# Sample index scores in four column groups, and two gate tiles moved from the sample steps into the index stage

## The reference, cut to what matters

```python
isc = jnp.einsum('bqhd,bkd->bqhk', qib, k_idx).astype(jnp.float32) * (IDX_DIM ** -0.5)
isc = jnp.einsum('bqhk,bqh->bqk', jax.nn.relu(isc), wib.astype(jnp.float32)) * (IDX_HEADS ** -0.5)
...
vals, idx = lax.top_k(isc, topk)
...
gates = jax.nn.sigmoid(gate_logit.reshape(b, t, N_BRANCH, D_MODEL))
merged = jnp.sum(gates * y, axis=2)
```

## Time and profile before

| | |
|---|---|
| median of 3 runs | 2609.43 us (2607.01 to 2613.8) |
| the profiled execution | 2608.09 us, its span 2606.2 us |
| PE busy | 2493.3 us, 96% of the span, 17084 matmuls |
| DVE, ACT, POOL busy | 1040.1, 566.1, 63.1 us |
| chain that ended last | PE 87%, DMA 6%, DVE 3%, ACT 2% |
| mean granted clock of PE | 0.988 of full |

### The profile page before, as it was taken

How to read it: one execution, slowest core, us unless ns; L and a number is a source line. 1 busy time by engine, 2 the same in 40 slices (tenths; PEclk the granted TensorE clock), 3 DMA queues, 4 the chain that set the end, 5 groups by cost and what they waited for, 6 DMA issues and landing times.

```text
span 2606.2 us, 40922 instructions
## 1 busy us (share of the span) xinstructions
PE 2493.3 (96%) x17084; PEld 2095.9 (80%) x17084; DVE 1040.1 (40%) x2388; ACT 566.1 (22%) x1262; POOL 63.1 (2%) x100
## 2 busy tenths in 40 slices
PE   7999999999999899999999999999999999999998
PEld 6999997656666589999989999965566665999997
DVE  3455202203676435554016660112066854266501
ACT  3000003114544322000021001120235442310101
POOL 0000000000012100000000000000000120000000
PEclk8999999999999999999999999999999999999998
DMA  8566421542369544665642232225414783323321
GB/s 300 186 226 216 165 89 51 143 136 70 110 224 298 166 148 162 227 225 176 219 142 89 98 120 89 94 67 139 130 61 159 254 283 129 130 73 122 109 89 69
DMA packets 299559, 389.92 MB, mean 150 GB/s; under 512 B 33677, under 2 KB 245385, under 8 KB 299378
## 3 DMA queue, kind: packets, MB, share of 16 engines
q1 hardware_dynamic: 281538, 339.52, 38.9%
q0 software_dynamic: 10752, 38.93, 4.6%
q10 hardware_dynamic: 7088, 8.87, 0.9%
HBM read 377.66 MB, written 9.62 MB: 149 GB/s over the span
## 4 chain that ended last, share of the span: by engine, by line
PE 87%; DMA 6%; DVE 3%; ACT 2%; SPq 1%; issue 1%; ACTq 0%; DVEq 0%; POOL 0%; POOLq 0%
PE PS L665 25%; PE PS L711 13%; PE PS L791 12%; PE PS L845 8%; PE PS L1037 4%; PE PS L592 3%; DMA QR<-w_ada 3%; PE PS L648 3%; PE PS L632 2%; PE PS L745 2%; PE PS L734 2%; PE PS L996 2%; PE PS L1059 2%; PE PS L1051 2%; PE PS L966 1%; PE PS L1006 1%
## 5 line engine op out<-in xcount | busy, mean ns | idle before, releaser
L711 PE MATMUL PS<-BIG,RING 128*128 128x192 f32 x2112 | 345.8, 326 | 0.0
L711 PEld LDWEIGHTS PS<-BIG,RING 128*128 128x128 f32 x2112 | 343.0, 190 | 1.5 <-issue 1.4
L791 PE MATMUL PS<-RING,H 128*128 128x384 f32 (+1 forms) x960 | 307.2, 482 | 0.0
L791 PEld LDWEIGHTS PS<-RING,H 128*128 128x128 f32 x960 | 181.8, 190 | 121.0 <-issue 0.6
L845 PE MATMUL PS<-H,RING 128*128 128x384 f32 x672 | 224.3, 488 | 0.0
L665 PE MATMUL PS<-OT,RING 128*128 128x192 f32 x1216 | 222.5, 326 | 0.0
L665 PE MATMUL PS<-H,RING 128*128 128x192 f32 x1216 | 213.8, 329 | 0.0
L665 PE MATMUL PS<-OT,QR 128*128 128x192 f32 x1216 | 210.0, 326 | 0.0
L665 PEld LDWEIGHTS PS<-H,RING 128*128 128x128 f32 x1216 | 199.0, 191 | 5.6 <-issue 5.4
L665 PEld LDWEIGHTS PS<-OT,RING 128*128 128x128 f32 x1216 | 201.8, 190 | 0.0
L665 PEld LDWEIGHTS PS<-OT,QR 128*128 128x128 f32 x1216 | 199.7, 190 | 0.0
(11 more groups left out here) (242 smaller groups left out, 3122.0 us busy)
## 6 DMA issues: line engine op xcount, KB each, us to landing
RING<-ffn_w_in SPq DMA_DIRECT2D x80, 1024.0 KB, 7.2
QR<-w_ada SPq DMA_DIRECT2D x66, 1024.0 KB, 9.4
RING<-w_in SPq DMA_DIRECT2D x64, 768.0 KB, 6.0
RING<-ffn_w_out SPq DMA_DIRECT2D x32, 768.0 KB, 4.6
RING<-ffn_w_out SPq DMA_DIRECT2D x32, 640.0 KB, 5.9
QKT<-cache_sb_k SPq DMA_DIRECT2D x16, 768.0 KB, 6.1
QR<-cache_sb_v POOLq DMA_DIRECT2D x16, 768.0 KB, 4.9
QKT<-cache_fox_k SPq DMA_DIRECT2D x16, 768.0 KB, 6.1
```

Source lines behind the costliest of these rows:

```text
L711: mm = pe.matmul(PS[:, m + 2 * g, 0:HALF], w[:, k, m * P:(m + 1) * P], HID[:, half * k2 + k, GROUP[g]], start=(half == 0 and k == 0), stop ...
L791: mm = pe.matmul(PS[:, n % 3, 0:width], H[:, k, tt * P:(tt + 1) * P], w[:, k, :], start=(k == 0), stop=(k == KD - 1))
```

## The change

`QIP` shrinks from 640 to 128 columns a head: only the 32 query columns of each pair are kept. The four pairs no longer add up in PSUM: each writes 32 PSUM partitions of its own (rows 32 bp to 32 bp + 32), with `start=True, stop=True`. The number of MATMULs stays 64 a layer. The result is the same 128 rows by 528 keys in the same banks.

Gate tiles 6 and 7 (`GATE_SCORE`) are now computed in the index stage, before heads 2 and 3 and behind their waits for the ReLU; ACT takes them after the ReLUs of heads 1 and 2. `prompt_scores(0)` comes after head 3, and behind a wait for tile 7 to be taken. All later tiles have numbers two higher in the prompt stage, in the same places; the sample steps have seven tiles instead of nine, in steps 0, 1, 2, 3, 5, 12 and 19 instead of 0, 1, 2, 3, 4, 6, 11, 17 and 22. `ROUND_S` and the loads stay as they are.

```diff
@@ -60,8 +60,9 @@
 GATE_FIRST = [0, 1, 2]
 GATE_INDEX = [3, 4, 5]
-GATE_PROMPT = [[6, 7, 8], [9, 10], [11], [12], [13], [14]]
-GATE_STEP = dict(zip((0, 1, 2, 3, 4, 6, 11, 17, 22), range(15, 24)))
+GATE_SCORE = [6, 7]
+GATE_PROMPT = [[8, 9, 10], [11, 12], [13], [14], [15], [16]]
+GATE_STEP = dict(zip((0, 1, 2, 3, 5, 12, 19), range(17, 24)))
@@ -188,7 +189,7 @@
-        QIP = qr(o, IH * 640).rearrange("p (h c) -> p h c", h=IH); o += IH * 640
+        QIP = qr(o, IH * P).rearrange("p (h i c) -> p h i c", h=IH, i=4); o += IH * P
@@ -909,14 +910,15 @@
                     if h >= 2:
                         pe.wait_ge(relu_ready, l * 6 + (h + 1))
+                        gate_tile(GATE_SCORE[h - 2], h - 2, 0)
                     for half in range(2):
                         for bp in range(4):
-                            mm = pe.matmul(PS[:, 4 + 2 * (h % 2) + half, 0:264], QIP[:, h, bp * P:(bp + 1) * P],
-                                           KIT[:, bp, half * 264:(half + 1) * 264], start=(bp == 0), stop=(bp == 3))
+                            mm = pe.matmul(PS[32 * bp:32 * bp + 32, 4 + 2 * (h % 2) + half, 0:264], QIP[:, h, bp, :],
+                                           KIT[:, bp, half * 264:(half + 1) * 264], start=True, stop=True)
                     mm.then_inc(is_ready, 1)
-                    if h == 2:
-                        prompt_scores(0)
-
+
+                pe.wait_ge(gate_taken, l * 24 + GATE_SCORE[-1] + 1)
+                prompt_scores(0)
@@ -1295,7 +1297,7 @@
-                        dst = QIP[s, h, :].rearrange("p (i c) -> p i c", c=160)[:, :, NT * par:NT * par + NT]
+                        dst = QIP[s, h, :, NT * par:NT * par + NT]
@@ -1320,6 +1322,8 @@
                           ACT.Relu, scale=1 / 16).then_inc(relu_ready, 1)
+                        if n in (3, 4):
+                            take_gate(GATE_SCORE[n - 3], n - 3)
```

## The result

The changed kernel takes 2631.76 us (median of 4 runs, 2625.38 to 2633.28) beside 2609.19 us for the kernel before on the same chip: ratio 1.0079, 95% interval 1.0058 to 1.0101. So it is slower by about 21 us, where 9 us was forecast and 2628 us was the end of the range. The profiled execution took 2633.28 us against 2608.09.

A forecast was written before the change was run, and what follows sets the result against it. The prediction took PE as the bound (87% of the chain). Terms 1 to 5 gave +2.1 us and term 6 +6.8, so +8.9 on 2608.09; with 1.3 for the runs' median, 2618 us, range 2606 to 2628.

The forecast's parts named there:

- The scores: Index stage: index scores in column groups take 0.9 us a head, 4.2 us a layer instead of 14.5.
- Term 1: Index stage: two tiles brought in, shorter scores and a 4.1 us wait for the ReLU; +4.25 us a layer.
- Term 2: Steps 4 to 7: uncovered top-k rounds delay `output` by 3.05 us in steps 5 and 7; +1.5 us a layer.
- Term 3: Steps 11 to 13: a tile covers step 12's round and mask, step 11's round shows; -0.5 us a layer.
- Term 4: Step 22: without its tile it takes 4.54 us instead of 8.21, like step 23; -3.7 us a layer.
- Term 5: Transfers in the sample steps: some stall saved at step 12, some added in steps 13 to 18; -0.5 us a layer.
- Term 6: PE's clock falls behind new pauses in the index stage and steps 5 and 7; +3.4 us a layer, +6.8 in all.
- Rival A: Forecast mechanics with the clock falling in the index stage and most step pauses; 2613 to 2625 us, chance 0.50.

The follow-up runs named there:

- e14: Changed kernel with discarded MATMULs filling the pauses of the index stage, of steps 5 and 7 and of the end; ratio 1.0022 to the kernel before.
- e4: Changed kernel with 12 discarded MATMULs put into the index stage's pause; ratio 1.0061 to the kernel before.
- e5: Changed kernel with 8 discarded MATMULs put into the pauses of steps 5 and 7; ratio 1.0057 to the kernel before.
- e2: Changed kernel with the top-k rounds of steps 4 and 6 moved under tiles in steps 0, 1 and 5; ratio 1.0033 to the kernel before.
- e16: Changed kernel run once more, unedited; ratio 1.0080 to the kernel before.
- e1: Changed kernel with tile 6 placed ahead of the wait for head 0's ReLU; ratio 1.0023 to the kernel before.
- e10: Changed kernel with tile 6 ahead of the ReLU wait and sample-step tiles in steps 0, 1, 2, 3, 4, 6, 22; ratio 0.9976 to the kernel before.
- e11: Changed kernel with the tile of step 19 moved to step 22; ratio 1.0073 to the kernel before.
- e12: Changed kernel with discarded MATMULs ahead of the values in step 22, in step 23 and after it; ratio 1.0069 to the kernel before.
- e6: Kernel before with the four column groups alone, no tile moved; ratio 0.9998 to the kernel before.
- e15: As e10, but with the seventh sample-step tile in step 17 instead of 22; ratio 0.9986 to the kernel before.

## Why the prediction was wrong, point by point

**The scores, right.** 0.9 us a head in column groups, 4.2 us in all: 1.99 us for two heads and 1.10 for each of the others, 4.2.

**Term 1, the wait: right in mechanism, 0.25 short.** A wait of 4.1 us forecast, 4.18 measured, released by the ReLU. Without the clock the stretch grows by 4.5 us (e14, e4) instead of 4.25.

**Term 2, the uncovered rounds: right.** Steps 4 to 7 are 29.9 us with the clock held up (e5, e14) where 1.5 on top of 28.7 make 30.2. The pause was 2.98 for 3.05. e2 shows it from the other side.

**Term 3: not resolved.** -0.3 / +0.5 for -0.5 in the first profile; over the eight profiles steps 8 to 13 are 34.6 to 35.9 us, 35.3 in the mean, beside 35.5 and 35.3 before.

**Term 4: the first step that failed.** Step 22 was priced by its look-alike, step 23, as if it waited for nothing else. It took 5.65 us in layer 0 instead of 4.54, held by the mask's transfer through DVE, and 6.26 in layer 1; its pause of 2.56 us was followed in layer 0 by 17 us at 0.50 instead of the 7 to 10 that the kernel before has there (layer 1: 3 and 7 us). Of 3.7 us a layer 0.5 and 1.1 were left in this profile, and less in others: in e16 the end is 20.5 and 21.1 us, longer than before, and over the six kernels that have the same end (changed, e16, e1, e2, e4, e5) it is 19.8 in the mean beside 19.7, with 0.6 us won in the branch products. I had looked at the clock only behind the three pauses that I had found, and not at those that a tile taken out leaves at the end.

**Term 5: right in the mean.** -0.8 / -1.2 in steps 14 to 21 of the first profile, 44.9 us in the mean of the eight beside 45.1 and 45.9: -0.6 for -0.5. But the view behind it was too mild. A tile there is worth about 2 us, not 4.6; e10 and e11 show it. For the change itself this costs little, because it has as many tiles in steps 8 to 21 as before, two. The prediction calls 351 GB/s the ceiling; the 389 GB/s from 718.3 to 722.0 show that more is possible, for some us at least.

**Term 6, the clock: the step that failed most.** Mechanism, places and sign were right, and the number of falls nearly so: 4.7 a kernel by the term (two, and 0.67 of four), 5.2 by the traces (14 of 14, and 19 of 24 of the short ones), six in the first profile. The size of a fall was not: I took 1.4 us in the index stage and 1.5 in the steps, from stretches of 3.3 us at 0.50. Measured in the first profile: 2.9 us in the index stage (8.36 for 5.43) and 2.7 and 2.6 in steps 5 and 7, with the clock at 0.50 in all of the 5.5 to 5.9 us read; in the mean of all profiles 2.6 and 2.2. That makes 16 us in the first profile and 12 in the mean, where the term has 6.8. The rows of before had longer falls too, at the ends of the sample steps; I read the six short ones and put the others into the upper end (+12) without weight. The Trainium skill (TensorE: Matmul & The Clock Gate, HAM oscillation) tells of a kernel in which the clock fell again behind every wait; by that, all six fall. Of the pauses here 33 of 38 did: a mean of 5.2 a kernel, no farther from my 4.7 than from six, and neither number makes 12 us without the larger price.

Put together: terms 1 to 5 gave +2.1, and e14, which takes most of the clock out, measures +5.7; the missing gain of term 4, 0.25 us a layer of term 1 and the two falls named below fill that. The clock has the rest, 15 us between e14 and the changed kernel: about 12 are term 6 at its true size, and about 3 are at the end of the sample steps (e12), where the prediction had no new fall. Rival A was the right case, with a price for the clock of little over half and nothing for the end.

What stays open: e14 still has falls at 723 and 2007, behind a pause of 2.0 us before the sample steps that the kernel before has as well and that brings none there. The fills aren't needed for it: e6 and e11, which have none, show the same fall in both layers, and the changed kernel and e16 in neither. Over all 14 profiles this pause brought 12 falls of 28. What decides between them isn't known, nor what decides between a fall of 1.5 us and one of 2.6.

## What to carry to other kernels

Before work is taken off the engine that bounds a kernel, look at what the other engines do under it: here a tile was the cover of two top-k rounds, and a score was long enough to hide a ReLU chain. A pause that is left on TensorE costs its own length and, behind it, up to 3 us more at half clock; put work that is ready into it (e1 won 15 us by moving one wait), and if there is none, even discarded matmuls pay. And where PE waits for transfers anyway, matmul work is cheap (about 2 us for a tile of 5): that is the place for movable tiles, not the place to take them from.

## What the runs showed of the hardware

- Four groups of 32 columns run together in float32: 32 MATMULs of 264 columns in 1.99 us, where the whole array took 3.63 us for 16. A head of 16 and the change to the whole array take 1.02 us where a second head adds 0.9, so the change costs about 0.1 us (an estimate).
- PE's clock fell to 0.50 behind 14 of 14 pauses of 4.2 us and 19 of 24 of 3.0 us, 12 of 28 of 2.0 us (before the sample steps), and one of two of 1.55 us (e2). It was at 0.50 in all of the 5.5 to 5.9 us read behind three pauses of the changed kernel, and in 16.9 us at the end of its sample steps.
- A fall costs 1.4 to 3.0 us, in steps 5 and 7 either 1.4 to 1.7 or 2.5 to 2.7. Filling a pause with matmuls to no purpose avoided it there (e4, e5, e12), and the work behind the filled pause did not start later (6.16 us after the first score in e4 as in the changed kernel).
- The same kernel's runs spread by 8 us in the first series (2625.38 to 2633.28) and by 19 in e16 (2621.13 to 2640.05), and its profiles differ in how many short pauses bring a fall.
- The transfers of steps 8 to 21 moved 306 to 316 GB/s with their engines at 0.96 to 0.99 (e10, e15); from 718.3 to 722.0 the kernel before moved 389 GB/s.
